# Level products of a chunked recurrence: inverse and level matrices on the other half of the partitions, two products in turn over four quadrants

## The reference

```
def step(state, inp):
    r_t, w_t, k_t, v_t, a_t, b_t = inp
    sa = einsum('bhvk,bhk->bhv', state, a_t)
    state = state * w_t + sa[..., None] * b_t + v_t[..., None] * k_t
    return state, einsum('bhvk,bhk->bhv', state, r_t)
```

## Time and profile before

| | us |
|---|---|
| median of three runs | 2718.99 |
| the runs | 2718.7, 2718.99, 2721.82 |
| span of the profiled execution | 2720.5 |
| PE busy | 2659.5 (98%) |
| DVE busy | 976.2 (36%) |
| the stage of the chunks (446 to 575 us) | 129.0 |

### The profile page before, as it was taken

How to read it: one execution, slowest core, us unless ns; L and a number is a source line. 1 busy time by engine, 2 the same in 40 slices (tenths; PEclk the granted TensorE clock), 3 DMA queues, 4 the chain that set the end, 5 groups by cost and what they waited for, 6 DMA issues and landing times.

```text
span 2720.5 us, 72988 instructions
## 1 busy us (share of the span) xinstructions
PE 2659.5 (98%) x33444; PEld 2258.5 (83%) x33444; DVE 976.2 (36%) x1863; ACT 365.0 (13%) x830; POOL 29.4 (1%) x47
## 2 busy tenths in 40 slices
PE   8999999899999999999999999999999999999998
PEld 8956778887677768867966688589999999999997
DVE  6662554623697333435664334320000000000002
ACT  1002232210100023400000342110000000000000
POOL 0000000000000000000000000010000000000000
PEclk9999999999999999999999999999999999999999
DMA  6445332013433433335345333479999999999996
GB/s 252 152 144 198 109 122 85 4 59 136 153 139 139 185 130 149 117 139 195 146 140 199 122 141 129 149 290 383 384 385 408 394 386 394 385 407 395 388 413 255
DMA packets 56915, 605.43 MB, mean 223 GB/s; under 512 B 6528, under 2 KB 6656, under 8 KB 11344
## 3 DMA queue, kind: packets, MB, share of 16 engines
q1 hardware_dynamic: 52272, 587.74, 55.2%
q0 software_dynamic: 4512, 15.77, 1.8%
HBM read 598.63 MB, written 4.86 MB: 222 GB/s over the span
## 4 chain that ended last, share of the span: by engine, by line
PE 92%; DVE 3%; DMA 2%; issue 1%; ACT 1%; POOL 0%; DVEq 0%; SPq 0%; ACTq 0%; POOLq 0%
PE bank L312 21%; PE bank L2671 21%; PE bank L468 10%; PE bank L2683 10%; PE bank L322 6%; PE bank L526 4%; PE bank L489 4%; PE bank L1787 3%; PE bank L500 3%; PE bank L1353 2%; DMA slot<-in_experts 2%; PE bank L1773 1%; DVE arena L1982 1%; PE bank L1081 1%; PE bank L1374 1%
## 5 line engine op out<-in xcount | busy, mean ns | idle before, releaser
L2671 PE MATMUL bank<-arena,slot 128*64 128x96 f32 x14336 | 614.2, 246 | 7.6 <-DMA slot<-in_experts 3.5
L2671 PEld LDWEIGHTS bank<-arena,slot 128*64 128x64 f32 x14336 | 599.9, 137 | 11.7 <-issue 11.5
L312 PE MATMUL bank<-h_cm,slot 128*128 128x256 f32 (+2 forms) x2032 | 446.7, 381 | 1.3 <-ACT h_cm L355 0.6
L312 PEld LDWEIGHTS bank<-h_cm,slot 128*128 128x128 f32 (+2 forms) x2032 | 382.2, 189 | 63.9 <-issue 9.7
L2857 DVE TENSOR_TENSOR ff<-ff,bank 128x192 f32<-128x192 f32 x112 | 39.7, 354 | 788.7 <-PE bank L2671 788.7
L2683 PE MATMUL bank<-ff,slot 128*64 128x96 f32 x7168 | 316.2, 246 | 1.3 <-issue 1.3
L2683 PEld LDWEIGHTS bank<-ff,slot 128*64 128x64 f32 x7168 | 304.4, 137 | 1.8 <-issue 1.8
L489 PE MATMUL bank<-h_cm,slot 128*128 128x256 f32 x704 | 154.9, 381 | 0.1
L489 PEld LDWEIGHTS bank<-h_cm,slot 128*128 128x128 f32 x704 | 134.6, 191 | 22.8 <-issue 4.8
L1982 DVE SCALAR_TENSOR_TENSOR arena<-arena 128x384 f32<-128x384 f32 x264 | 142.7, 613 | 1.2
L2809 ACT ACTIVATE ff<-bank 128x192 f32<-128x192 f32 x112 | 37.0, 330 | 759.8 <-PE bank L2671 759.8
(11 more groups left out here) (444 smaller groups left out, 2318.4 us busy)
## 6 DMA issues: line engine op xcount, KB each, us to landing
slot<-in_experts SPq DMA_DIRECT2D x112, 2048.0 KB, 8.7
slot<-in_experts SPq DMA_DIRECT2D x112, 1024.0 KB, 8.6
slot<-in_ffn SPq DMA_DIRECT2D x22, 2048.0 KB, 9.1
slot<-in_ffn SPq DMA_DIRECT2D x22, 1024.0 KB, 4.9
slot<-in_dense SPq DMA_DIRECT2D x11, 2048.0 KB, 7.6
slot<-in_dqk SPq DMA_DIRECT2D x8, 2048.0 KB, 7.6
slot<-in_g SPq DMA_DIRECT2D x8, 2048.0 KB, 7.5
slot<-in_w_in_rkv SPq DMA_DIRECT2D x6, 2048.0 KB, 7.7
```

The lines of the kernel that those rows point to most:

```text
L312: ins = pe.matmul(ps[0:m, j * S:(j + 1) * S], w[:, k * width + c0:k * width + c0 + m], rhs[:, k, :], start=k == 0, stop=k == ks - 1)
L2671: ins = pe.matmul(bank[64 * c:64 * c + 64, m * PLACES:(m + 1) * PLACES], slot[s][:, c0:c0 + 64], queue[:, k, :], start=k == 0, stop=k == K ...
```

## The change

The plain product is computed twice per head and chunk: once as before, but written to the other half of the partitions, and once with its operands exchanged, which gives the transpose, on its own half. One masking instruction per p now writes level 0 of both TI and TT, which lie side by side (`BOTH`), and one addition adds the identity to both. The first quarter of the key products (x = 0, the matrix from which AM is masked) is written to the other half too. So AM and TI of a chunk lie on the half of the other chunk; TT, X1 and all else stay. The left-hand step and X2 therefore have operands on one half and results on the other (`across`, the two quadrants off the diagonal), and XT stays on the diagonal. The right-hand step of levels 1 to 4 takes both banks first and issues, head by head, two matmuls of X2 and two of XT. TT's level 0 is no longer masked out of the key products.

```diff
@@ -896,6 +896,7 @@
         TI, TT, AM0, AM1 = ([xflat[:, (4 * a + i) * 256:(4 * a + i + 1) * 256].rearrange("p (h i s) -> p h i s", h=2, i=2)
                              for a in range(2)] for i in range(4))
         AM = [AM0, AM1]
+        BOTH = [xflat[:, a * 1024:a * 1024 + 512].rearrange("p (m h i s) -> p m h i s", m=2, h=2, i=2) for a in range(2)]
         ff_flat = ff[:, :, :].rearrange("p n s -> p (n s)")
         X1, XV = ([ff_flat[:, (2 * a + i) * 256:(2 * a + i + 1) * 256].rearrange("p (h i s) -> p h i s", h=2, i=2)
                    for a in range(2)] for i in range(2))
@@ -1354,6 +1355,14 @@
                                         start=True, stop=True)
                 return ins
 
+            def across(ps, a, h, left, right):
+                p, i = HEADS[h]
+                for c in range(2):
+                    rows = chunk_rows(c)
+                    ins = pe.matmul(ps[chunk_rows(1 - c), h * 64:h * 64 + 64], left(rows, a, p, i), right(rows, a, p, i),
+                                    start=True, stop=True)
+                return ins
+
             def head_of(src, g):
                 t, k0 = PAIRS[g[0]]
 
@@ -1371,7 +1380,7 @@
                     for i in range(2):
                         for c in range(2):
                             tok, k = chunk_tokens(t, c), k0 + 2 * a + i
-                            ins = pe.matmul(ps[chunk_rows(c), (2 * x + i) * 64:(2 * x + i + 1) * 64],
+                            ins = pe.matmul(ps[chunk_rows(c if x else 1 - c), (2 * x + i) * 64:(2 * x + i + 1) * 64],
                                             left[rows, k, tok], right[rows, k, tok], start=True, stop=True)
                 filled(ins, ("LM", j, a, p))
 
@@ -1383,8 +1392,12 @@
                 for i in range(2):
                     for p, c in QUADRANTS:
                         rows, tok, k = slice(64 * p, 64 * p + 64), chunk_tokens(t, c), k0 + 2 * a + i
-                        last[p] = pe.matmul(ps[p][chunk_rows(c), i * 64:(i + 1) * 64], DEC[rows, k, tok], KK[rows, k, tok],
-                                            start=True, stop=True)
+                        pe.matmul(ps[p][chunk_rows(1 - c), i * 64:(i + 1) * 64], DEC[rows, k, tok], KK[rows, k, tok],
+                                  start=True, stop=True)
+                    for p, c in QUADRANTS:
+                        rows, tok, k = slice(64 * p, 64 * p + 64), chunk_tokens(t, c), k0 + 2 * a + i
+                        last[p] = pe.matmul(ps[p][chunk_rows(c), P + i * 64:P + (i + 1) * 64], KK[rows, k, tok],
+                                            DEC[rows, k, tok], start=True, stop=True)
                 for p in range(2):
                     filled(last[p], ("LB", j, a, p))
 
@@ -1401,8 +1414,10 @@
                 if l > 1:
                     drained(pe, ("X2", j, a, l - 1))
                 ps = fill(pe, ("X1", j, a, l), next_bank())
-                filled(by_chunk(ps, a, 64, 0, lambda rows, a, p, i: AM[l % 2][a][rows, p, i, :],
-                                lambda rows, a, p, i: TI[a][rows, p, i, :]), ("X1", j, a, l))
+                for h in range(len(HEADS)):
+                    ins = across(ps, a, h, lambda rows, a, p, i: AM[l % 2][a][rows, p, i, :],
+                                 lambda rows, a, p, i: TI[a][rows, p, i, :])
+                filled(ins, ("X1", j, a, l))
 
             def level_right(g, l):
                 j, a = g
@@ -1410,12 +1425,19 @@
                 if l > 1:
                     drained(pe, ("XT", j, a, l - 1))
                 if l < 5:
-                    ps = fill(pe, ("X2", j, a, l), next_bank())
-                    filled(by_chunk(ps, a, 64, 0, lambda rows, a, p, i: TT[a][rows, p, i, :],
-                                    lambda rows, a, p, i: X1[a][rows, p, i, :]), ("X2", j, a, l))
+                    ps2 = fill(pe, ("X2", j, a, l), next_bank())
                 ps = fill(pe, ("XT", j, a, l), next_bank())
-                filled(by_chunk(ps, a, 64, 0, lambda rows, a, p, i: X1[a][rows, p, i, :],
-                                lambda rows, a, p, i: TT[a][rows, p, i, :]), ("XT", j, a, l))
+                for h, (p, i) in enumerate(HEADS):
+                    if l < 5:
+                        ins2 = across(ps2, a, h, lambda rows, a, p, i: TT[a][rows, p, i, :],
+                                      lambda rows, a, p, i: X1[a][rows, p, i, :])
+                    if l < 5 and h == len(HEADS) - 1:
+                        filled(ins2, ("X2", j, a, l))
+                    for c in range(2):
+                        rows = chunk_rows(c)
+                        ins = pe.matmul(ps[rows, h * 64:h * 64 + 64], X1[a][rows, p, i, :], TT[a][rows, p, i, :],
+                                        start=True, stop=True)
+                filled(ins, ("XT", j, a, l))
 
             def solved(g):
                 j, a = g
@@ -1620,6 +1642,7 @@
                 for t in range(T):
                     drained(dve, ("tm", name, t, 0))
             heads4 = [P, 2, 2, CHUNK]
+            both_level0 = const("level0", 2 * CHUNK).rearrange("p (m s) -> p m s", m=2).unsqueeze(2).broadcast_to(heads4)
 
             def each_head(mask):
                 return const(mask, CHUNK).unsqueeze(1).unsqueeze(1).broadcast_to(heads4)
@@ -1641,17 +1664,16 @@
                 j, a = g
                 for p in range(2):
                     ps = full(dve, ("LB", j, a, p))
-                    free(nc.vector.tensor_tensor(TI[a][:, p, :, :], ps[:, 0:128].rearrange("p (i s) -> p i s", s=CHUNK),
-                                                 times(const("level0", CHUNK), 2), ALU.mult), ("LB", j, a, p))
+                    free(nc.vector.tensor_tensor(BOTH[a][:, :, p, :, :], ps[:, 0:256].rearrange("p (m i s) -> p m i s", m=2, i=2),
+                                                 both_level0, ALU.mult), ("LB", j, a, p))
 
             def level_zero(g):
                 j, a = g
                 for p in range(2):
                     drained(dve, ("LM", j, a, p))
                     drained(dve, ("LB", j, a, p))
-                ch.add(nc.vector.tensor_tensor(TT[a], LM[a][:, :, 0, 0, :, :], each_head("levelT0"), ALU.mult))
-                ch.step(nc.vector.tensor_tensor(TI[a], TI[a], each_head("eye"), ALU.add))
-                ch.step(nc.vector.tensor_tensor(TT[a], TT[a], each_head("eye"), ALU.add))
+                both = BOTH[a].rearrange("p m h i s -> p (m h i) s")
+                ch.step(nc.vector.tensor_tensor(both, both, times(const("eye", CHUNK), 8), ALU.add))
                 mask_level(j, a, 1)
 
             def level(g, l):
```

## The result

The changed kernel takes 2810.68 us (median of 4 runs) against 2718.84 us for the kernel before on the same chip: ratio 1.0341, with a 95% interval of 1.0325 to 1.0356. It is slower by 92 us, where 2712.4 us was forecast, and outside of the range.

The account below looks back on a forecast made before the run. PE carries 92% of the chain, but VectorE sets the pace in the middle of a stage turn. 2720.5 - 7.6 + 1.0 = 2713.9, carried to the runs' median as 2712.4 us; 8 in 10 between 2709.0 and 2717.5.

Parts of the forecast that it names:

- Downstream: Behind the recurrence stage (575 us): everything waits on PE or its slots, gain let through whole; clock shift taken as 0.
- Instruction supply: In or behind the outputs: pauses that look like late instructions grow, costing 1.0 us, bounds 0 and 2.8 us.
- the five pauses: Pauses without a semaphore in the stage's loop, in or behind the outputs: 0.56, 0.67, 0.29, 0.40 and 0.74 us.
- rival A: Instruction supply takes most: pauses grow with each fast block, 4.2 us of the loop's gain goes; 2715.6 us; chance 0.20.
- Points 3 and 4: Right-hand steps of new levels 1 and 2, each turn: faster over four quadrants, -0.20 and -0.40 us.
- B: Rival for the right-hand steps: four quadrants don't run together, 29 ns a record stays; about 2719 us; chance 0.08.
- C: Rival for the right-hand steps: interleaving serialises, 58 ns a record, 0.93 us more a step; 2747 us; chance 0.05.
- the ends: Before and behind the stage's loop: shorter right-hand steps of levels 1 and 2, then 3 and 4; -0.70 and -0.80 us net.
- Point 2: VectorE's queue, each turn: -1.25 removed, +0.72 and +0.26 added, net -0.27 us, all on the path.
- Point 5: Second plain products, each turn: 16 records more, +0.23 us on PE, hidden where PE waits for VectorE, 0 on the path.
- Rival D: The clock falls inside the stage's loop as PE's idle stretch grows, some 1.8 us a fall; 2715 to 2722 us; chance 0.05.
- The stage of 122 to 123 us: Sign that the forecast was right: the recurrence stage, 129 us before, at 122 to 123 us.

Follow-up runs that it names:

- repaired kernel: The changed kernel with twelve 64 x 64 products of constants (48 records) ahead of the expert stage: 2730.11 us, ratio 1.0027 to the kernel before.
- the run without it: The changed kernel with 48 records of padding and the right-hand step issued as before, all of X2 and then all of XT: ratio 1.0007.
- both mergings: The kernel before with key products and query products that share weights issued as one of double width, 768 records less: 2714.69 us, ratio 0.9971.
- the burst: The kernel before with 256 products of 64 x 64 constants (1,024 records), in turn over four quadrants, ahead of the expert loop: 2736.24 us in one run.
- the merged keys: The kernel before with the four key products of a head and chunk issued as two of double width, 512 records less: 2719.97 us, ratio 0.9989.

## Why the prediction was wrong

Two steps of the prediction failed: "Downstream", by far the larger, which missed 82 us, and "Instruction supply", which took the gain itself.

- **"Instruction supply"** saw the five pauses and read them rightly as late instructions, but bounded their growth by the 0.40 us of one step and turn: 1.0 us, at most 2.8. Against the 4.88 us of the kernel before they were 12.66 in the repaired kernel, **+7.8**, which is the whole gain of 7.6. Outside its pauses that stage did get shorter, by 8.0 us (123.98 to 115.97). What was late was not one step's instructions but each block's: whatever PE saves inside a block that is used up too fast comes back at its end.
- **"Downstream"**, put at 0, looked at waits, slots and one fall of the clock, and never at the code itself. The 280 records that the change puts into the program were counted as time (+0.23 hidden, rightly) and not as a shift of what lies behind them. That cost 82 of the 87 us of the profiles: six times the reload at the head of a turn, with the clock that fell behind it. No rival held this one; rival A priced the supply of the stage alone, at 3.4 us of gain left where nothing was.
- **Points 3 and 4, and B and C:** the step over four quadrants takes 0.47 to 0.48 us on two shared banks, as forecast (level 3's, behind products of one row half, mostly 0.63); B and C fall. Its worth by the run without it is 3.2 us of the stage, where the forecast had 6.1 (0.60 a turn and 1.86 at the ends).
- **Point 2** was right in its two terms and wrong in the sum: a wait for the plain products takes most of the 0.27.
- **Point 5**, hidden plain products: right to within 0.7 us of the stage, when put in alone.
- **Rival D** came true beside the rest: two falls inside the stage of the kernel after, none in the same stage of the kernel with 12 products. What decided that between two stages of the same code was not tried.
- The stage of 122 to 123 us that was to show success didn't come: 133.14, and 128.63 with the padding. The kernel before with both mergings has 123.13, but that is another gain, of fewer records, and speaks neither for nor against the change.

## What to carry to other kernels

Look at the queue of instructions as at any other: where PE's records are short, count how long a block of 256 takes, and near the 3.5 to 3.8 us of the burst don't count on a gain from faster records; fewer and wider ones pay, since two products with the same weights are one. An edit ahead of a hardware loop moves its code: if the packets of the instruction queue jump, here from 103 to 158, try a few dozen records of padding before reading anything else. And a forecast for one stage has to ask what every later loop does with the code's new place.

## What the runs showed of the hardware

- **Blocks of 256.** PE's instructions come in packets of 16.4 KB, and the pauses stand 256 records apart. The Trainium skill, Runtime: NRT & Kernel Launch, Instruction fetch mechanics, gives 16 KiB blocks of 256 instructions, and the runs agree.
- **A floor per block.** In the burst, 3.5 to 3.8 us a block for 2.1 us of work: 1.1 us until the next packet starts, 0.9 to 1.3 for the packet, 1.3 to 1.4 until PE goes on. It binds only once the blocks loaded ahead are used up, as the first 234 products show. In the stages of the kernels above at most two of some 27 blocks were done in under 3.0 us, and the blocks with a pause behind them took 3.5 to 4.0 us on the mean. The same section calls the crossing of a block mostly hidden, as instructions are dispatched more slowly than they come. For records of 64 x 64 on four quadrants, 14.6 ns for a matmul with its weights counted as two records of 7.3, the burst shows the contrary.
- **A loop fits or is loaded again.** The expert loop is 1,574 records of code, counted between the marks of its branches in the trace. In the kernel after, a turn's first 15 records stand ahead of a block's start (the 6 matmuls at 2036.83, their weight loads and 3 register records), six blocks take 1,536 more, and the last 23 records lie in an eighth block. In the kernel before all lies 24 records earlier, and the loop ends one record short of that block: seven in all. The kernel after loads 9 blocks in each later turn, which takes 126.3 us instead of 112.1; the kernel before loads none. The count rests on the records that the trace shows, so it may be off by one or two; places between these two were not tried. The section gives PE 2048 instructions, eight blocks, but also calls it only two cache lines and says that a jump outside the current two pages has to be fetched. By two pages the loop of seven blocks would be loaded again in each turn, and it isn't; how many blocks PE held was not measured.
- **Idle time that the supply makes also costs clock.** The granted clock was 0.72 of full over 12 us at the head of each loop turn, and 0.63 over 9 us behind the burst.
- **Left open:** runs of one kernel spread over up to 13 us (the kernel before from 2718.5 to 2731.6 in one comparison), while the stage of the same code lies within 0.7 us in three traces (128.75, 128.86 and 129.44). The rest of the kernel spreads, and it hides part of what the stage gains: -4.1 us of stage gave -0.11% with the merged keys, -5.7 gave -0.29% with both.
